# Gates, key products and the merged block inversion inside the in-projection; the conditioning tiles of the in-projection's last stage moved to the out-projection

## The reference

```python
cond = silu(c); mod = cond @ ada_w[i] + ada_b[i]        # 6 pieces of 2048: sh1, sc1, g1, sh2, sc2, g2
h = rmsnorm(x, w0) * (1 + sc1) + sh1
proj = h @ in_w                                         # 2048 -> 8192 (q,k,v) + 4096 (z) + 128 (gates ba)
q, k, v = silu(short_conv(proj[qkv]));  q, k = l2norm(q), l2norm(k)      # 16 q/k heads, 32 v heads
beta = sigmoid(ba[0]);  g = -exp(A_log) * softplus(ba[1] + dt_bias);  g = cumsum(g) in chunks of 64
decay = exp(g_i - g_j)                                  # inside a chunk, i >= j
lower = strict_lower((k*beta) @ k.T * decay)            # 64 x 64
u, w = solve(eye + lower, [v*beta, k*beta*exp(g)])      # then a scan over the 4 chunks with state S
o = o_forward + o_backward;  o = rmsnorm(o, norm_w) * silu(z);  h = o @ out_w
x = x + (1 + g1) * rmsnorm(h, w1);   h = rmsnorm(x, w2) * (1 + sc2) + sh2;   x = x + (1 + g2) * rmsnorm(swiglu(h), w3)
```

## Time and profile before

| | us |
|---|---|
| median of 3 runs | 3550.8 |
| the profiled execution's own time | 3550.19 |
| its span, first to last instruction | 3548.3 |
| q, k, v slices | 130.0 to 513.0 |
| z slices | 513.0 to 734.6 |
| end of z to the second head of the attention | 734.6 to 917.7 |
| out-projection | 1298.5 to 1475.0 |

### The profile page before, as it was taken

One profiled execution on the slowest core, in us unless ns is written; L12 is line 12 of the kernel. 1 busy time (PEld: TensorE's weight loads), 2 busy tenths in 40 slices (PEclk: granted clock), 3 DMA queues, 4 the chain that ended last, 5 costly groups with the idle time before them and its releaser, 6 DMA issues.

```text
span 3548.3 us, 39044 instructions
## 1 busy us (share of the span) xinstructions
PE 2938.7 (83%) x13702; PEld 2438.5 (69%) x13702; DVE 2448.3 (69%) x2263; ACT 1405.7 (40%) x1379; POOL 410.3 (12%) x371
## 2 busy tenths in 40 slices
PE   1699999940777769799999999776638799999998
PEld 1588888830566658678888888665427688888886
DVE  7588888856677634587878778669985655555555
ACT  0267543420355443433333333445434433333333
POOL 0001002333333300000000000024430000000000
PEclk9899999965799879999999999888869899999999
DMA  9466778931564535488888888433214566565563
GB/s 363 182 232 235 243 260 320 379 111 62 96 95 95 74 121 194 154 327 313 324 321 312 314 322 334 135 125 107 95 48 154 199 213 204 201 213 201 201 213 130
DMA packets 337017, 729.19 MB, mean 206 GB/s; under 512 B 48960, under 2 KB 81808, under 8 KB 311088
## 3 DMA queue, kind: packets, MB, share of 16 engines
q1 hardware_dynamic: 331584, 708.67, 58.8%
q0 software_dynamic: 5360, 19.57, 1.5%
HBM read 708.49 MB, written 19.69 MB: 205 GB/s over the span
## 4 chain that ended last, share of the span: by engine, by line
PE 70%; DVE 15%; issue 5%; DMA 4%; ACT 4%; DVEq 1%; SPq 0%; POOL 0%; ACTq 0%; POOLq 0%
PE psg L627 41%; PE psg L633 21%; DVE y L1449 4%; DMA aring<-in_ada_w 2%; PE pst L788 1%; PE psn L654 1%; DVE wraw L1311 1%; ACT dec L1719 1%; DMA wraw<-in_gdn_in_w 1%; PE pst L616 1%; DVE sinv L379 1%; DVE aacc L1016 1%; DVE stmp L374 1%; DVE wlo L1006 1%; DVE aacc L1102 1%
## 5 line engine op out<-in xcount | busy, mean ns | idle before, releaser
L1006 DVE TENSOR_TENSOR wlo<-wraw,whi 128x2048 fp32r<-128x2048 f32 x441 | 1018.4, 2310 | 581.3 <-ACT whi L1532 579.5
L1532 ACT ACTIVATE whi<-wraw 128x2048 fp32r<-128x2048 f32 x441 | 844.7, 1916 | 1345.9 <-PE psg L633 1218.2
L627 PE MATMUL psg<-whi,h_hi 128*128 128x512 f32 (+1 forms) x2592 | 821.4, 399 | 28.5 <-DVE h_lo L1492 13.0
L627 PE MATMUL psg<-whi,h_lo 128*128 128x512 f32 (+1 forms) x2592 | 808.9, 394 | 0.0
L633 PE MATMUL psg<-wlo,h_hi 128*128 128x512 f32 (+1 forms) x2592 | 659.7, 398 | 99.6 <-DVE wlo L1006 99.6
L633 PEld LDWEIGHTS psg<-wlo,h_hi 128*128 128x128 f32 x2592 | 498.1, 194 | 208.4 <-DVE wlo L1006 105.7
L627 PEld LDWEIGHTS psg<-whi,h_hi 128*128 128x128 f32 x2592 | 493.6, 193 | 133.1 <-issue 21.7
L627 PEld LDWEIGHTS psg<-whi,h_lo 128*128 128x128 f32 x2592 | 496.5, 192 | 104.2
L1016 DVE SCALAR_TENSOR_TENSOR aacc<-aring,cond,aacc 128x2048 f32<-128x2048 f32 x153 | 366.1, 2393 | 5.1 <-DMA aring<-in_ada_w 4.7
L627 PE MATMUL psg<-whi,g_hi 128*128 128x512 f32 x704 | 219.2, 393 | 0.0
L627 PE MATMUL psg<-whi,g_lo 128*128 128x512 f32 x704 | 219.0, 392 | 0.0
(11 more groups left out here) (213 smaller groups left out, 2747.7 us busy)
## 6 DMA issues: line engine op xcount, KB each, us to landing
aring<-in_ada_w SPq DMA_DIRECT2D x192, 1024.0 KB, 7.0
wraw<-in_ffn_in_w SPq DMA_DIRECT2D x176, 1024.0 KB, 6.4
wraw<-in_gdn_in_w SPq DMA_DIRECT2D x97, 1024.0 KB, 5.3
wraw<-in_ffn_out_w SPq DMA_DIRECT2D x88, 1024.0 KB, 5.2
wraw<-in_cf_pw_w SPq DMA_DIRECT2D x48, 1024.0 KB, 5.1
wraw<-in_gdn_out_w SPq DMA_DIRECT2D x32, 1024.0 KB, 5.0
rr<-d_rows SPq DMA_DIRECT2D x16, 1024.0 KB, 15.2
d_qkn<-kn POOLq DMA_DIRECT2D x8, 512.0 KB, 3.5
```

The source lines that it names most:

```text
L627: mm(ps[:, t, 0:width], a[:, kc, t * P:(t + 1) * P], wh, start=first and j + n == 0, stop=False)
L1006: tt(wlo[:, j % 2, :], wraw[:, j % 4, :], whi[:, j % 2, :].bitcast(F32), SUB).then_inc(w_lo, 1)
L1532: av(whi[:, j % 2, :], wraw[:, j % 4, :], ACT.Copy).then_inc(w_hi, 1)
```

## The change

Five things move.

1. The gates are computed in q slices 0 and 1 (`gate_a` to `gate_d`, the matmuls `gate_sums` after the third tile, `gate_rows` after the fourth). The rows go to DRAM by POOL's queue, a second time in an order per head (`d_rr`), so that `load_rr` reads one contiguous 8 KB row. The block decays follow at the end of slice 1, in the buffer of `x` (which is loaded again from DRAM afterwards); their Exp stands on ScalarE after slice 9.
2. The key products are formed at the end of slices 10 to 13, into the PSUM tensor `psn`, and evacuated in the next slice after `evac`; TensorE waits for that evacuation (`kk_ev`) at the head of slices 11 to 14.
3. The inversion works on all four blocks in one instruction (the backward direction is stored transposed), all on VectorE, in pieces of a budget of 2800 ns behind the `lo` of the z tiles 4 to 24. The product of the first head (`kq`) is formed in z slice 7.
4. The z tiles bring no conditioning tiles. These 32 tiles go to the out-projection: two behind each of tiles 4 to 7, one behind each of tiles 8 to 31, with `fin` after tile 15 and after the last tile.
5. Buffers: `inv` and `rr` of the attention lie in weight slots 3 and 2, `exb` has a buffer of its own; `d_inv` is stored in six pieces. The sum into `t64` is two instructions where it was one.

```diff
-            for part, z0 in ((3, 0), (4, 4)):
...
-                            load_w(G_Z + 4 * zs + j, (G_Z + j) % 4, rows4(gdn_in, j * KT * P, QKV + zs * NSL))
-                            load_ada(48 + 4 * zs + j, aring, (0, part), 8 * i + 4 * s + j)
...
+            for z in range(NZ):
+                for j in range(4):
+                    load_w(G_Z + 4 * z + j, (G_Z + j) % 4, rows4(gdn_in, j * KT * P, QKV + z * NSL))
...
+            load_rr(0)
+            sp.wait_ge(c_v, C_INV)
+            for part, to in ((slice(0, 16), inv_out0), (slice(16, P), inv_out)):
+                for (s0, s1), src in (((2, 6), sinv[:, :]), ((6, 8), sdec[:, 0:2]), ((0, 2), sdec[:, 2:4])):
+                    sp.dma_start(d_inv[part, s0:s1].rearrange("p s i j -> p (s i j)"),
+                                 src[part].rearrange("p s i j -> p (s i j)")).then_inc(to, 16)
+            sp.wait_ge(c_init, C_CONST + 1)
+            sp.wait_ge(inv_out0, 48)
+            load_inv(0)
...
+            sp.wait_ge(inv_out, 48)
+            sp.dma_start(x[:, :, :], x_in[0].rearrange("(t p) d -> p t d", p=P)).then_inc(x_land, 16)
...
+            def load_ada2(m):
+                load_ada(48 + m, aring2, (0, 3 + m // KC), m % KC)
             for j in range(1, 8):
                 load_w(G_GO + j, (G_GO + j) % 4, rows4(gdn_out, j * KT * P, 0))
-            with sp.Fori(1, 4) as n:
+                if j == 3:
+                    sp.wait_ge(osp_lo, 8)
+                if j >= 4:
+                    load_ada2(2 * j - 8)
+                    load_ada2(2 * j - 7)
+            for n in range(1, 4):
                 for j in range(8):
                     load_w(G_GO + 8 * n + j, (G_GO + j) % 4, rows4(gdn_out, j * KT * P, n * NSL))
+                    load_ada2(8 * n + j)
...
+        def invert(count, js):
+
+            work = sinv[:, :]
+            for j in js:
+                n, m = 31 - j, j + 1
+                shape = [P, 4, n, m]
+                tmp = stmp[:, :, 0:n * m].rearrange("p c (i k) -> p c i k", k=m)
+                to = work[:, :, m:32, 0:m]
+                count.wait(nc.vector)
+                count.inc(nc.vector.tensor_tensor(tmp, sdec[:, :, m:32, j].unsqueeze(3).broadcast_to(shape),
+                                                  work[:, :, j, 0:m].unsqueeze(2).broadcast_to(shape), MUL))
+                count.wait(nc.vector)
+                count.inc(nc.vector.tensor_tensor(to, to, tmp, ADD))
...
+            for s in range(10, NQKV):
+                if 11 <= s <= 14:
+                    pe.wait_ge(kk_ev, 4 * (s - 10))
+                qkv_slice(s, s % 2, "v")
+                if s < 14:
+                    kk(s - 10)
...
+            left = list(range(31))
+            for n in range(4 * NZ):
+                lo(G_Z + n, G_Z + n)
+                if n < 2:
+                    decay_kk((2 * n, 2 * n + 1))
+                elif n < 4:
+                    conv(NQKV - 1, 1, (2 * n - 4, 2 * n - 3))
...
+                if n >= 4 and left:
+                    budget = 2800
+                    while left and budget > 0.6 * (160 + 8 * (31 - left[0]) * (left[0] + 1)):
+                        j = left.pop(0)
+                        invert(pr, (j,))
+                        budget -= 160 + 8 * (31 - j) * (j + 1)
...
+            def qkv_slice(s, par, kind, kk=None):
...
+                def a1():
+                    evac(s - 1, 1 - par)
+                    if kk is not None:
+                        kk_evac(kk)
```

More of the change, by code:

```diff
@@ new lines, in build @@
+        h_lo = sb("h_lo", [P, KC, T], F32R, at=p1)
+        p1.close()
+        gates = ExitStack()
+        bt = sb("bt", [P, 3, TT, P], at=gates)
+        rowsT = sb("rowsT", [P, TT, P], at=gates)
+        rows = sb("rows", [P, T], at=gates)
+        srow = sb("srow", [P, 8, 32], at=gates)
+        tri = sb("tri", [P, 4, P], at=gates)
+        gates.close()
+        inner = ExitStack()
+        skk = sb("skk", [P, 32, 32], at=inner)
+        inner.close()
+        ada_st.close()
+        inner = ExitStack()
@@ L207, in build @@
         oms = sb("oms", [P, 3, 4], at=p2a)
+        free_slot = wraw[:, (G_GO + 3) % 4, :].rearrange("p (a b c m) -> p a b c m", a=2, b=4, c=TT)
+        wt = free_slot[:, 0]
+        assert (G_GO + 1) % 4 == 2 and (G_GO + 3) % 4 == 0
+        uu = free_slot[:, 1].rearrange("p b c m -> p (b c m)").rearrange("p (o c m) -> p o c m", o=2, c=4)
+        rr = wraw[:, 2, :].rearrange("p (c t) -> p c t", t=T)
+        inv = wraw[:, 3, :].rearrange("p (s t m) -> p s t m", s=8, t=TT)
+        sb("apart", [P, 756], at=p2a)
+        oT = sb("oT", [P, HV, T], at=p2a)
         p2a.close()
@@ L353, in build, with slot_of @@
         C_G, C_ROWT, C_ROWS, C_SUB, C_DEC = 5, 13, 14, 17, 21
-        C_INV = C_DEC + 2 * (2 * 31 + 1)
-        C_POOL = 22
-        C_POOL_INV = C_POOL + 2 * 31 + 1
+        C_INV = C_DEC + 2 * 31 + 2
+        C_TRI, C_SINV, C_CONST = 5, 7, 22
         block = stack.enter_context(nc.Block())
[L360 to L382, removed]
+        def slot_of(a, c):
+            return 4 * a + (c + 2) % 4
+        def invert(count, js):
[10 more added lines that the diff above has]
+                count.inc(nc.vector.tensor_tensor(to, to, tmp, ADD))
         def rows4(w, r0, n0):
@@ new lines, in gate_d, with decay @@
+            def gate_d():
+                dve.wait_ge(c_p, 2)
+                pr.inc(nc.vector.tensor_copy(rows[:, :], psn[:, 2, :]))
+                assert pr.n == C_ROWS
+            def decay():
+                dve.wait_ge(s_land, 16)
+                dve.wait_ge(sq_ok, TT)
+                sr4 = srow[:, :, :].rearrange("p (c k) i -> p c k i", k=2)
+                for d in range(2):
+                    pr.inc(tt(sdec[:, 2 * d:2 * d + 2],
+                              sr4[:, 2 * d:2 * d + 2, 0, :].unsqueeze(3 - d).broadcast_to([P, 2, 32, 32]),
+                              sr4[:, 2 * d:2 * d + 2, 1, :].unsqueeze(2 + d).broadcast_to([P, 2, 32, 32]), SUB))
+                pr.wait(dve)
+                sflat = sdec[:, :, :, :].rearrange("p c i j -> p (c i j)")
+                pr.inc(ts(sflat, sflat, 0.0, None, MIN))
+                assert pr.n == C_SUB
@@ L1157, in _ @@
                     qkv_slice(2 + 2 * i + s, s, True)
-            def z_slice(z, par, n, lag=False, extra=None):
-                for j in range(4):
-                    lo(G_Z + 4 * z + j, G_Z + j)
-                    if lag and j >= 2:
-                        conv(NQKV - 1, 1, (2 * j - 4, 2 * j - 3))
-                    if extra and j == 0:
-                        extra()
-                    ada(48 + 4 * z + j, j % 2, aring, aacc[:, n, :], (4 * z + j) if isinstance(z, int) else z * 4 + j - 16)
```

558 lines of the change are left out of this document (283 added, 275 removed).

## The result

The changed kernel takes 3430.16 us (median of 4 runs, 3425.74 to 3434.32) beside 3550.98 us of the kernel before: ratio 0.966 (95% interval 0.9642 to 0.9677), 121 us less. The forecast was 3403, 147 less, in a range of 3382 to 3432. The direction held, and so did the mechanism behind z; one term of the sum was wrong by a whole slice. The profiled execution took 3434.32 us (span 3432.7), 115.9 less than the one of before.

A forecast was written before the change was run, and what follows sets the result against it. TensorE was taken to bound q, k, v, z slices 2 to 7 and the out-projection, with a serial stretch behind z. The terms summed to −147.2 us, from 3550.2 to 3403, range 3382 to 3432.

The forecast's parts named there:

- The stretch behind z: From z's end to the attention's second head: serial work leaves, 21.2 us in place of 183.1, −161.9.
- A merged step: Inversion on VectorE in z: two instructions per step, 8.3nm ns + 0.2; 31 steps about 53 us, ending near tile 24.
- Key products: Slices 10 to 13: TensorE waits for their evacuation at the next slice's first tile, then runs slower; +24, bounds 7 and 32.
- decays: End of slice 1: 6.8 us new on VectorE make the next `lo` late and TensorE slow; +5, bounds 0 and 8.
- z: z slices without conditioning tiles and key products: 187 us in place of 221.6, −34.6, mostly from slices 0 and 1.
- Rival A: Out-projection becomes bound by loads and the ring of two: 20 to 30 us more, 3423 to 3433; chance 0.14.
- Out-projection: Conditioning tiles moved there: 8 for tiles 4 to 7, 6.6 for the middle fold, 2.5 for single late loads; +17.1 without the −4.
- Attention: The step into `t64` as two instructions: +0.14 per head, × 16 = +2.2; no wait expected for `inv` and `rr`.
- the −4 behind it: Out-projection's start: three weight loads in flight in place of four and more shorten the load on the chain, −4 us.
- rival D: Attention: `rr` lands late, paid 16 times; priced at a landing of 30 us, +160, about 3563, slower than before; chance 0.02.
- The small terms of gates and Exp: Gates in slices 0 and 1 with two more small loads, +3.6; decays' Exp on ScalarE after slice 9, +1.4.
- rival B: Merged inversion steps in z cost more than separate ones, through strided operands or POOL's storing beside them: +40, 3443; chance 0.06.

The follow-up runs named there:

- the second set of runs: The changed kernel measured once more, unedited, as the base of the other runs: 3432.5 us, ratio 0.9654 to the kernel before.
- experiment 3: Changed kernel with TensorE's wait for the key products' evacuation moved to where `psn` is next written, after the slice's second tile: 3413.1 us, ratio 0.9599.
- experiment 7: Changed kernel with the three VectorE operations of the block decays placed one each at the end of slices 1, 2 and 3: 3423.5 us, ratio 0.9627.
- experiment 1: Kernel before with the conditioning products in z cut to 8 of 2048 columns: 3543.9 us, ratio 0.997; z 189.3 us for 198.2.
- experiment 6: Changed kernel with the two transposing copies behind the inversion split over the next two z tiles: 3423.1 us, ratio 0.9631; z 183.8 us for 190.1.
- experiment 4: Changed kernel with the out-projection's conditioning tiles spread, one per weight tile from tile 4, a second only at 10, 16, 22, 28: 3425.0 us, ratio 0.9633.
- experiment 5: Changed kernel with each out-projection weight load issued one tile earlier, ahead of the conditioning loads: 3426.6 us, ratio 0.9641.
- experiment 8: Changed kernel with wait moved, copies and decays split, conditioning tiles spread, weight loads ahead, first head's q and k load earlier: 3396.8 us, ratio 0.9554.

## Why the prediction was right in direction, and too large

The saving of 121 us lies inside the range, and its largest part came as reasoned. That the time does so, 1.8 us from the range's upper end, is in part luck: the room there had been left for the rivals, and a miscounted window used it up. The profiled execution (3434.3) and the second set of runs (3432.5) lie above 3432.

- The stretch behind z: right, 159.3 of 161.9. A merged step by itself cost what the sum said (1.21 us for 1008 elements, about 1.1 ns each with the fixed part 0.1). All 62 instructions took 66.7 us, not 53 (the sum's own fixed part is 31 × 0.2 = 6.2, not 7.1): some 11 of the difference, by my estimate, are eleven of them that ran beside a GpSimd product and took about 1.0 longer each. The steps ended at 711.0 and the copies at 715.4, 41 us before z's end, so it cost nothing behind z.
- Key products and decays: right to 0.2 us each, with the idle of 2.64, its slow tile and the late `lo`. Experiments 3 and 7 take them back by their causes.
- z: wrong, −7.9 for −34.6. The step that failed is the length of z before, "221.6 now", with "slices 0 and 1, which lose 27.7": the window held the last v slice, and z took 198.2. With the right border the same reasoning gives 198.2 to 187, and a total of 3426. Experiment 1 measures the disputed gain by itself: 9, not 27. Of the 26.7 that the term was off 23.4 are the border; the other 3 are less than what the block of copies cost (6.3, experiment 6). Rival A's "for" rested on the same 27.7.
- Out-projection: +19.7 for +17.1. Mechanism right (VectorE's 7.0 in 5.44, the ring, the fold: 4.5 + 2.3), the stall 12.4 for 8 (11.0 in the repeated run), since SP's order adds to VectorE's excess: neither edit alone takes the stalls away, both together do (experiments 4, 5, 8). The 2.5 for single late loads did not show. So rival A was there in a mild form.
- Attention: the pair of instructions into `t64` takes 1.29 us for 1.22, half of the forecast's +0.14 per head. Second to last head took 309.0 for 309.5; with 308.6 to 311.1 in the other kernels of this attention, the +2.2 can't be told. Nor can the −4 behind it: last head to out-projection takes 71.3 us before, 68.6 after, and 68.2 in experiment 1, where nothing was changed there. What of VectorE's work is on a head's path there was not tried. `rr` lands in 5.3 as `cwb` did, so rival D is out.
- The small terms of gates and Exp were 3.5 too high.

## What to carry to other kernels

Count the tiles in a window before taking its length as a stage's: a window can be full of the neighbour's work and look like a loss. A wait belongs where the buffer is next written, not at the head of the slice: here that was 16 us (experiment 3). Work fitted into slack must be cut to the slack of one tile, each block of it (copies, decays, second tiles), and a load that a later step waits for must not stand in an in-order queue behind one that waits for a busy engine.

## What was not expected of the hardware

A step of the inversion on VectorE that ran beside POOL's product for z took about 1.0 us longer whatever its size: 2.31 for 1.22 at 1020 elements, and 1.26 at 124 elements (the last row of the steps in experiment 6) where 240 elements took 0.41 without it. POOL's product took 4.66 for 2.48. VectorE in the changed kernel, then POOL (a product beside the steps, and one alone):

```profile
644.15 2.31 DVE L378 TENSOR_TENSOR skk<-x,sinv 128x1020 f32<-128x1020 f32 x1
646.50 2.20 DVE L381 TENSOR_TENSOR sinv<-sinv,skk 128x1020 f32<-128x1020 f32 x1
...
655.41 1.22 DVE L378 TENSOR_TENSOR skk<-x,sinv 128x1020 f32<-128x1020 f32 x1
```

```profile
642.96 4.66 POOL L2024 TENSOR_TENSOR zw<-ev,gwb 128x512 f32<-128x512 f32 x2 [16.36 <-issue]
...
757.93 2.48 POOL L2024 TENSOR_TENSOR zw<-ev,gwb 128x512 f32<-128x512 f32 x2 [12.55 <-ACT ev L1689]
```

That is what the Trainium skill, "SBUF — State Buffer", section "SBUF: two separate sides", says of two inputs in SBUF against a GpSimd read: the one waits for the other's whole instruction. The 1.0 to 1.1 fit: one of POOL's two instructions takes 1.26 alone. It cost 2.1 us in one tile per slice, and VectorE's slack took it up where nothing else stood in that tile: rival B in small. The second: while the stores of the inverse blocks were in flight, SP took 2 to 3.7 us for the issue of a 32 KB load that it otherwise issues in 0.45.
